# Sums of the context tokens' value rows: all on TensorE in column groups, at other places beside the main work

## What is computed

```python
def block(args):
    xb, ib, gb = args
    act = jax.nn.gelu(jnp.einsum('td,thkd->thk', xb, u_tab[ib]), approximate=False)
    return jnp.einsum('thk,thkd->td', gb * act, v_tab[ib])
```

## Time and profile before

| | us |
|---|---|
| median of 3 runs | 3764.92 (3758.97 to 3766.16) |
| the profiled execution | 3768.37 |
| its span, first to last instruction | 3766.6 |
| PE busy | 3291.4 (87%) |
| DVE busy | 2851.2 (76%) |
| POOL busy | 1375.1 (37%) |
| ACT busy | 928.8 (25%) |

### The profile page before, as it was taken

One profiled execution on the slowest core, in us unless ns is written; L12 is line 12 of the kernel. 1 busy time (PEld: TensorE's weight loads), 2 busy tenths in 40 slices (PEclk: granted clock), 3 DMA queues, 4 the chain that ended last, 5 costly groups with the idle time before them and its releaser, 6 DMA issues.

```text
span 3766.6 us, 32345 instructions
## 1 busy us (share of the span) xinstructions
PE 3291.4 (87%) x9441; PEld 1672.5 (44%) x9441; DVE 2851.2 (76%) x6490; ACT 928.8 (25%) x2415; POOL 1375.1 (37%) x1205
## 2 busy tenths in 40 slices
PE   7678989987897988577777789999999999999998
PEld 4355434433543444234433444444454444444444
DVE  2637797659767878888898589888787888777776
ACT  1322221355422111146634501011011101110111
POOL 1000554546654445333233222333333333333331
PEclk9889999999998999788998899999999999999999
DMA  9243876768888899999999999999999999999996
GB/s 349 76 176 132 291 247 224 256 221 297 298 307 309 297 346 333 393 360 360 337 396 383 370 365 396 386 404 403 409 411 411 416 391 404 416 409 409 407 409 271
DMA packets 305103, 1269.03 MB, mean 337 GB/s; under 512 B 29456, under 2 KB 79888, under 8 KB 218656
## 3 DMA queue, kind: packets, MB, share of 16 engines
q0 software_dynamic: 169200, 959.16, 65.8%
q1 hardware_dynamic: 134000, 302.17, 21.5%
q10 hardware_dynamic: 1728, 5.64, 0.4%
HBM read 1217.28 MB, written 49.58 MB: 336 GB/s over the span
## 4 chain that ended last, share of the span: by engine, by line
PE 26%; issue 23%; DVE 22%; DMA 19%; POOL 7%; ACT 3%; SPq 0%; DVEq 0%; POOLq 0%; ACTq 0%
DMA arena<-in_uv,idx 7%; DMA ring_e<-in_uv,idx 6%; PE bank L902 5%; PE bank L930 3%; PE wide L845 3%; DMA ring_e<-in_v_rows,idx 3%; PE bank L1064 3%; DVE arena L1873 3%; POOL arena L791 3%; POOL ring_e L791 2%; DVE ring_e L1873 2%; DVE ring_e L1813 2%; PE wide L1114 2%; DVE arena L1904 2%; PE bank L1094 2%
## 5 line engine op out<-in xcount | busy, mean ns | idle before, releaser
L791 POOL DMA_INDIRECT arena<-in_uv,idx x384 | 454.8, 1184 | 845.8 <-PE bank L1126 506.1
L1169 PE MATMUL bank<-arena 128*128 128x384 f32 x2048 | 695.7, 494 | 55.8 <-ACT arena L1569 34.6
L1873 DVE CUSTOM_DVE_ANT_0 arena<-arena,h2e 128x1024 f32<-128x1024 f32 x384 | 460.8, 1220 | 150.3 <-DMA arena<-in_uv,idx 149.3
L1169 PEld LDWEIGHTS bank<-arena 128*128 128x128 f32 x2048 | 392.2, 193 | 370.2 <-issue 136.4
L791 POOL DMA_INDIRECT ring_e<-in_uv,idx x256 | 296.2, 1157 | 618.4 <-PE bank L1126 350.8
L750 POOL DMA_INDIRECT ring_e<-in_u_rows,idx x256 | 330.7, 1292 | 486.7 <-DVE dots_e L1813 332.5
L1182 PE MATMUL wide<-arena 128*128 128x512 f32 x1024 | 462.2, 594 | 5.6 <-DVE arena L1943 5.5
L1512 ACT ACTIVATE small<-small 128x4 f32<-128x4 f32 x160 | 32.7, 205 | 1416.8 <-DVE small L1873 1416.8
L1873 DVE CUSTOM_DVE_ANT_0 ring_e<-ring_e,h2e 128x1024 f32<-128x1024 f32 x256 | 306.8, 1219 | 85.1 <-DMA ring_e<-in_uv,idx 84.9
L1813 DVE CUSTOM_DVE_ANT_0 ring_e<-ring_e,h2e 128x1024 f32<-128x1024 f32 x256 | 303.1, 1219 | 50.6 <-DMA ring_e<-in_u_rows,idx 48.6
L845 PE MATMUL wide<-ring_e,diag_e 128*128 128x512 f32 x520 | 258.7, 638 | 83.4 <-ACT diag_e L1236 55.4
(11 more groups left out here) (265 smaller groups left out, 4424.4 us busy)
## 6 DMA issues: line engine op xcount, KB each, us to landing
arena<-in_ut SPq DMA_DIRECT2D x128, 512.0 KB, 7.9
arena<-in_uv SPq DMA_DIRECT2D x128, 512.0 KB, 8.3
arena<-in_w_q SPq DMA_DIRECT2D x48, 512.0 KB, 6.8
spread_d<-arena SPq DMA_DIRECT2D x12, 2048.0 KB, 25.4
arena<-spread_d SPq DMA_DIRECT2D x96, 256.0 KB, 10.7
ring_e<-in_w_mod POOLq DMA_DIRECT2D x16, 1024.0 KB, 8.1
arena<-in_w_cols SPq DMA_DIRECT2D x24, 512.0 KB, 5.5
arena<-in_x SPq DMA_DIRECT2D x20, 512.0 KB, 4.6
```

The costliest lines, as they stand in the source:

```text
L791: pool.indirect_dma_start(out=ring[r], out_offset=None, in_=a["uv"], in_offset=bass.IndirectOffsetOnAxis(ap=idx[kept(t)][:, k:k + 1], axis ...
L1169: ins = pe.matmul(s_bank[:, 0:NC], lhsT=utb[i % URING][:, k * P:(k + 1) * P], rhs=H2T[1][:, k, P:P + NC], start=(k == 0), stop=(k == KD - 1))
L1873: dve.tensor_tensor_reduce(out=ring[r][:, 0:D], in0=ring[r][:, 0:D], in1=h2b[kept(t)], scale=1.0, scalar=0.0, op0=ALU.mult, op1=ALU.add, a ...
```

## The change

Each slot now holds 32 tokens with four of their experts each: partition 32s + t of a slot has an expert s of token t. `idx` and the gates are written in that order by 16 pieces of 32x32 for each context tile, and the start signal `idx_ready` comes behind the places and no longer behind the gates. The rows of the tokens, `h2e`, are loaded by blocks of 32 tokens, four times over (`load_tokens`). A sum is then a product with a 128x32 matrix (`sel32`, a sum of the identity's columns, times the weights): four matmuls for a slot, one for each quarter of the 1024 columns, into partitions 32j to 32j + 31 of `wide[tile]`. All 256 slots are summed so; the sums on DVE are gone.

The pairs stand at the sites by a new table: 20 in `conv`, 11 in `qk`, 20 in `vg`, 4 in `ln`, 5 in `gates`, 9 in `states`, 6 in `attn`, 18 in `out`, 17 in `qf0`, 18 in `qf1`. A site may have none or two. PE sums the pairs of earlier sites, in the query rounds those of two rounds back.

Since the sums lie in PSUM by quarters, the end of tiles 0 and 1 changes: the residual rows, the gate and the final gain are loaded by quarters, the squares are summed by quarter on ACT, and PE adds the quarters (`fold_squares`).

```diff
-        for phase, n, vector in (("conv", 16, (False, True)), ("qk", 9, (False,)), ("vg", 16, (False, True)),
-                                 ("ln", 8, (False,)), ("gates", 8, (False,)), ("states", 14, (False,)),
-                                 ("attn", 10, (False,)), ("out", 16, (True,)), ("qf0", 16, (True,)), ("qf1", 16, (True,))):
...
+        for phase, sites, pairs in (("conv", 16, 20), ("qk", 9, 11), ("vg", 16, 20), ("ln", 8, 4), ("gates", 8, 5), ("states", 14, 9),
+                                ("attn", 10, 6), ("out", 16, 18), ("qf0", 16, 17), ("qf1", 16, 18)):
+            hooks[phase] = len(pairs_to) - 1
+            first = pairs_to[-1]
+            pairs_to += [first + pairs * (i + 1) // sites for i in range(sites)]
...
+        def pairs_before(phase, n):
+            return pairs_to[max(0, hooks[phase] + n - (phase in ("qf0", "qf1")))]
@@ POOL
-            for t in range(2):
-                pool.dma_start(h2e[t], h2_d[t * P:(t + 1) * P, :]).then_inc(*S["h2e_in"].mark(0, 16))
+            def load_tokens(n):
+                for i in range(4):
+                    pool.dma_start(h2e[n % 2][i * Q:(i + 1) * Q, :], h2_d[n * Q:(n + 1) * Q, :]
+                                   ).then_inc(*S[f"h2e_in{n % 2}"].mark(n, 16))
...
+                if k % Q == ERING - 1 and k > Q and k < (2 * SLOTS) - Q:
+                    load_tokens(k // Q + 1)
@@ PE
-            def early(s, phase, n):
-                c = hook(s, phase, n) - 1
...
-                for k in range(EC * c, EC * c + EC):
-                    if vector_sums(k):
-                        continue
+            def early(s, phase, n, upto=None):
...
+                upto = pairs_before(phase, n) if upto is None else upto
+                first, summed[0] = summed[0], max(summed[0], upto)
+                for k in range(EC * first, EC * summed[0]):
                     pe.wait_ge(*S["diag_e"].at(k))
                     pe.wait_ge(*landed_v[k % ERING].at(k))
-                    for h in range(2):
-                        ins = pe.matmul(wide[k // SLOTS][:, h * 512:(h + 1) * 512], lhsT=diag_e[k % ERING],
-                                        rhs=ring_e[k % ERING][:, D + h * 512:D + (h + 1) * 512],
-                                        start=(k % SLOTS == 0), stop=(k % SLOTS == SLOTS - 1), skip_group_check=True)
+                    c0 = k // Q % 4 * (D // 4)
+                    for j in range(4):
+                        ins = pe.matmul(wide[k // SLOTS][j * Q:(j + 1) * Q, c0:c0 + D // 4], lhsT=diag_e[k % ERING][:, 0:Q],
+                                        rhs=ring_e[k % ERING][:, D + j * (D // 4):D + (j + 1) * (D // 4)],
+                                        start=(k % Q == 0), stop=(k % Q == Q - 1), skip_group_check=True)
                     ins.then_inc(*S["used_e"].mark(k))
...
+            def fold_squares(t):
+                pe.wait_ge(*S["y_sum"].at(t))
+                bk = bank(("fold", t))
+                for j in range(4):
+                    ins = pe.matmul(bk[j * Q:(j + 1) * Q, 0:4], lhsT=sel32, rhs=fss[:, 0:4], start=True, stop=True,
+                                    skip_group_check=True)
+                full(ins, ("fold", t))
@@ ACT
-                    act.activation(diag_e[r0 + j], ident[:], ACT.Copy, scale=wts_e[:, r0 + j:r0 + j + 1]
+                    act.activation(diag_e[r0 + j][:, 0:Q], sel32, ACT.Copy, scale=wts_e[:, r0 + j:r0 + j + 1]
                                    ).then_inc(*S["diag_e"].mark(k0 + j))
@@ DVE
+                        if tile < STREAMS[0][1]:
+                            for g, s in quarters:
+                                done(dve.scalar_tensor_tensor(out=idx[p][s, g], in0=pi[0][g, s], scalar=float(NKEYS),
+                                                              in1=pi[1][g, s], op0=ALU.mult, op1=ALU.add))
+                            after()
+                            dve.sem_inc(S["idx_ready"].sem)
...
             def early(s, phase, n):
-                c = hook(s, phase, n)
-                if c >= 0:
-                    early_sums(c - 1)
+                for c in pairs_at(s, phase, n):
                     early_dots(c)
```

192 lines of the change are left out of this document (123 added, 69 removed).

## The result

The changed kernel takes **3815.31 us** (median of 4 runs, 3806.77 to 3821.71), the kernel before beside it 3763.24 us (3758.97 to 3766.16): a ratio of **1.0138 [1.0113, 1.0163]**. The forecast was 3713 us, between 3660 and 3765, with a chance of 0.10 for slower. The profiled execution took 3818.98 us, 50.6 more than the one of before.

A forecast was written before the change was run, and what follows sets the result against it. No single engine: from 350 to 1520 us the bound changes by stage (PE or DVE), then DMA. Terms sum to -52 us from the profiled 3768.4, which lies 3.5 above the median 3764.9, giving 3713; range 3660 to 3765.

The forecast's parts named there:

- a visit: On PE: one change from projections to column groups and back, priced at 0.36 us on top of 0.86 a pair.
- Gates and scan: Gates -7 us for three pairs of dots fewer on DVE; scan -12 us for five pairs fewer.
- Projections, -31 forecast: Projections: 720 us instead of 751.7, between -41 (no waits for v gathers) and 0 (every pair late).
- Eleven sites get two pairs: Projections: a v gather waits for the slot four before and takes 6.0 us to land; 9 us allowed.
- A second step: Projections' first part: DVE is the limit; with its sums gone it ends near 500 us, not 519.7.
- Query rounds, +22 forecast: Query rounds: +43.3 us of PE work, less 13.4 of waits and some 8 of clock; between +5 and +43.
- the rival of the ring: Query rounds: v gathers wait for sums two pairs back, so rounds last a gather and a sum; 3793 us, chance 0.07.
- Attention, -14 forecast: Attention: PE's chunk falls from 8.17 to 5.4 us, taken as 6.8; -14, between -26 and +5 (half the clock).
- Output, +16 forecast: Output: PE sums 17 pairs in 16 visits, 20.4 us, less 3.4 and the wait of the pair summed there now.
- Gap before the query rounds, -10 forecast: Before the query rounds: DVE no longer trails, so the 20.4 us shrink to about 10.
- The overlap: Column groups on PE overlap less: 1.30 us a pair, 3758 us; none at all, 3978. Chance 0.10, of it 0.03 none.
- The gathers as a matter of bandwidth: Projections: at 290 GB/s the gathers end at 780 us and the gain there is gone; 3744 us, chance 0.12.

The follow-up runs named there:

- e7: e1 with every sum of the query rounds issued twice, the second time with zero weights of the same form; 3783.62 us.
- e1: The changed kernel with at most one pair at a place, in the numbers the kernel before has; 3767.81 us, ratio 1.0016 to the kernel before.
- e12: The changed kernel with a slot's v gather behind one younger u gather in POOL's queue instead of two; 3782.18 us.
- e4: The changed kernel with a double place's second pair summed half a unit later in projections, output and query rounds, pair numbers unchanged; 3793.83 us.
- e9: The changed kernel with its sums one place later in conv, qk and vg; 3797.46 us.
- e12b: The changed kernel with a slot's v gather right behind its own u gather, with no younger u gather ahead; 3798.32 us.
- e5: e1 with three matmuls of zero weights added on TensorE behind each slot's sum, in the attention only; 3767.41 us.
- e8: e1 with sums one place later in conv, qk, vg and out, plus one zero-weight matmul behind each slot's sum in gates, scan and attention; 3744.81 us.

## Why the prediction was wrong

**Right.** The price of a pair, 0.86 us, and of a visit (1.20 less 0.86, so 0.34) held in the trace and in e7's. Gates and scan moved as worked out from VectorE's dots: e1, with the old number of pairs, has their old lengths (68.3 and 91.7). LayerNorm's -14.6 comes for the most part from the cheaper sums on PE: e1, with its old eight pairs, already has -12.7, so moving pairs away accounts for some 2 of it.

**Projections, -31 forecast, +15.** The step that failed is "Eleven sites get two pairs ... I allow 9 us for that". There were 26.5 us of waits for v rows, and 17 us of clock on the projections' own matmuls behind the waits (597 to 635 ns in the first part, where the granted clock is 0.89; 600 to 609 in the second). I priced the landing, 6.0 us, but not the queue ahead of it: two younger u gathers, at about 1.25 us an issue, back to back. e12 shows that order at work and e4 the bunching. That TensorE's clock falls in a wait for rows and the matmuls behind it start at the low one is also what the Trainium skill says in "TensorE: Matmul & The Clock Gate", section "HAM oscillation — how this bites in real kernels"; the row at 421.62, 9.45 us for 7.13, agrees. A second step failed with it, and the runs do not make it the smaller one: the 22.3 us of waits for diagonals before were taken for VectorE's lateness, which would go. They stayed at 26.6, since PE asked for a sum before ScalarE could have weighed it; a place's delay on the changed kernel (e9) takes 19 us of them and 32 off the stage, the order of the gathers (e12) takes 12 off it, half a unit between the pairs (e4) 15. These three were not tried together, so how the 46 us divide between the two steps stays open.

**Query rounds, +22 forecast, +44.** "Of its present waits 13.4 are for ScalarE's copies ... those go, and with them some 8 of the 11 us" of clock. They went, 7.3 of them behind the stage as the table counts it, so that the miss is 14 us by the forecast's own count (+36). 18.4 us for v rows in the rounds with two pairs took their place, and the projections' matmuls there went from 607 to 617 ns instead of gaining. It looks like the rival of the ring at three rounds of 32; but with the same four slots these waits are 10.3 us in e12 and none in e12b, so the order of the queue has the larger part. With single rounds e1 has +17.9, where the forecast's own prices make +16 for its 31 pairs.

**Attention, -14 forecast, -5.** "In the middle of the attention PE runs without a pause" was read as a bound. By the traces it was not the only one: a ring of ScalarE and VectorE of the same 8.2 us stands beside it, and PE's shorter chunk did not shorten that. The limits of -26 and +5 were drawn round PE alone, and +5 does not follow from half the clock either: 5.4 us doubled is 10.8 a chunk, which is +26 for ten. e1, with all ten pairs, is 7 us longer than before.

**Output, +16 forecast, +24.** The places with two pairs cost 5.1 us of waits for v rows and 1.6 for a diagonal, where e1's stage has 0.8 in all, and two pairs more cost 2. The clock is another matter: the 256 projection matmuls have a mean of 622 ns instead of 601 (5.4 us), but e1 has 621 with one pair at a place. The forecast had no such term, so that e1's +16.3 agrees with +16 partly by luck.

**Gap before the query rounds, -10 forecast, -2.** This is not v rows. The last place of the output has two pairs too, and VectorE's dots of the second wait for u rows; ScalarE's Gelu waits for the dots, its copies stand behind the Gelu, and PE waits for the copies:

```profile
1210.44 1.23 DVE L1872 CUSTOM_DVE_ANT_0 ring_e<-ring_e,h2e 128x1024 f32<-128x1024 f32 x1 [3.64 <-DMA ring_e<-in_u_rows,idx]
...
1211.70 0.20 ACT L1258 ACTIVATE gel_e<-dots_e 128x2 f32<-128x2 f32 x1 [4.88 <-DVE dots_e L1872]
...
1213.47 3.64 PE L843 MATMUL bank<-ident,arena 128*128 128x128 f32 x16 [11.12 <-ACT arena L1481]
```

In e1, with one pair there, that wait of PE is 5.1 us instead of 11.1 and the gap has the forecast's -8.0; e4, which leaves the dots where they are, keeps the gap at 18.3.

**The rivals.** The overlap is refuted. The gathers as a matter of bandwidth are too: the two parts of the projections moved 262 and 299 GB/s at shares of 0.75 and 0.88, where the scan of before moves 345 at 0.95, and e9 and e12 made them faster with the same rows. The gathers were late in their queue, which this rival did not have. Its price did not follow from its own sum: an end at 780 us lies 28 behind the old 751.7, which makes some 3772, not 3744.

## What to carry to other kernels

A price per unit of work is safe to multiply only where the work's inputs arrive at that rate: before two units go to one place, follow the queue that fetches them (issues, what stands in front of each, slots) through that place, not on average. An engine that runs without a pause need not be the bound; look whether two others wait for each other with the same period. An input that is asked for too early can cost as much as one that comes late: here asking one place later shortened the projections more than any other run that kept the change's pairs there. And when a stage seems to pay for a change, try first the cheap order knobs beside it on both kernels: here one number in a queue brought the old kernel to where the change stands at its best.

## What was not expected of the hardware

An indirect gather of one slot holds POOL for 0.94 us, now and then 1.7, with 0.30 to the next; around a place with two pairs that is all of POOL's time. Work with zero weights keeps TensorE's clock up at no loss in time, and gave back little: 1.2 us of the attention for 24 us of work and a clock of 0.94 instead of 0.81 (e5), 3.6 us for 8 us of work and 0.86 (e8).
